# Banded attention: where the small broadcasts and the value splits stand in a unit

## The reference

```python
q = rmsnorm(q.reshape(bsz, t, 8, 64), q_norm)         # the same for k; v is taken as it is
s = einsum('bnqhd,bnkhd->bnhqk', qc, kb) * 64 ** -0.5 + bias   # own chunk + 8 chunks before it
p = softmax(where(valid, s, -1e30))
o = einsum('bnhqk,bnkhd->bnqhd', p, vb)
```

## Time and profile before

| | us |
|---|---|
| median of three runs | 1673.1 |
| lowest, highest | 1669.12, 1678.57 |
| profiled execution, its own time | 1667.27 |
| its span, first to last instruction | 1665.5 |
| TensorE busy | 1583.8 (95%) |
| DVE busy | 983.7 (59%) |
| ACT busy | 657.9 (40%) |
| GpSimd (POOL) busy | 305.2 (18%) |
| mean granted TensorE clock | 0.977 |

### The profile page before, as it was taken

One profiled execution on the slowest core, in us unless ns is written; L12 is line 12 of the kernel. 1 busy time (PEld: TensorE's weight loads), 2 busy tenths in 40 slices (PEclk: granted clock), 3 DMA queues, 4 the chain that ended last, 5 costly groups with the idle time before them and its releaser, 6 DMA issues.

```text
span 1665.5 us, 27534 instructions
## 1 busy us (share of the span) xinstructions
PE 1583.8 (95%) x11220; PEld 1550.6 (93%) x11220; DVE 983.7 (59%) x1393; ACT 657.9 (40%) x1154; POOL 305.2 (18%) x354
## 2 busy tenths in 40 slices
PE   6999999997889999997889989999999999999999
PEld 6999999996788899997779989999999899999999
DVE  6626776536778643245643486666666558646653
ACT  5521021126889522124532263333333333333332
POOL 1011000002320010003410014444444411010110
PEclk9999999988999999998999999999999999999999
DMA  7425111002110244101051223443333686354563
GB/s 241 146 90 169 42 39 39 26 1 93 37 37 33 70 156 142 39 14 51 26 183 67 78 78 145 146 145 145 145 145 147 235 295 213 91 170 147 158 211 112
DMA packets 63666, 189.37 MB, mean 114 GB/s; under 512 B 7872, under 2 KB 13048, under 8 KB 63408
## 3 DMA queue, kind: packets, MB, share of 16 engines
q1 hardware_dynamic: 37904, 91.11, 17.3%
q0 software_dynamic: 25648, 96.65, 16.3%
HBM read 138.58 MB, written 54.12 MB: 116 GB/s over the span
## 4 chain that ended last, share of the span: by engine, by line
PE 84%; DVE 5%; DMA 4%; ACT 3%; issue 3%; POOL 1%; SPq 0%; DVEq 0%; ACTq 0%; POOLq 0%
PE ps L454 33%; PE ps L2700 19%; PE ps L2721 17%; PE ps L2228 3%; PE ps L2476 3%; PE ps L483 2%; DMA a<-wdn 2%; PE ps L2599 2%; PE ps L2416 1%; PE ps L2454 1%; DVE scores L1800 1%; PE ps L505 1%; PE ps L2567 1%; PE ps L2383 1%; DVE t_lo L2083 1%
## 5 line engine op out<-in xcount | busy, mean ns | idle before, releaser
L454 PE MATMUL ps<-A_hi,w_hi 128*128 128x364 f32 x768 | 173.5, 334 | 0.0
L454 PE MATMUL ps<-A_lo,w_hi 128*128 128x364 f32 x768 | 170.3, 330 | 0.0
L454 PE MATMUL ps<-A_hi,w_lo 128*128 128x364 f32 x768 | 170.0, 329 | 0.0
L395 DVE TENSOR_TENSOR w_lo<-w_raw,w_hi 128x1024 fp32r<-128x1024 f32 x43 | 52.5, 1223 | 152.5 <-ACT w_hi L391 152.0
L391 ACT ACTIVATE w_hi<-w_raw 128x1024 fp32r<-128x1024 f32 x42 | 44.3, 1057 | 242.3 <-PE ps L454 136.3
L454 PEld LDWEIGHTS ps<-A_lo,w_hi 128*128 128x128 f32 x768 | 134.8, 190 | 0.0
L454 PEld LDWEIGHTS ps<-A_hi,w_lo 128*128 128x128 f32 x768 | 134.0, 189 | 0.0
L454 PEld LDWEIGHTS ps<-A_hi,w_hi 128*128 128x128 f32 x768 | 133.6, 190 | 0.0
L2700 PE MATMUL ps<-t_hi,wq_hi 128*128 128x272 f32 x480 | 100.1, 290 | 4.1 <-DVE hid_stage L2124 4.1
L2700 PE MATMUL ps<-t_lo,wq_hi 128*128 128x272 f32 x480 | 99.7, 289 | 0.0
L2700 PE MATMUL ps<-t_hi,wq_lo 128*128 128x272 f32 x480 | 99.6, 289 | 0.0
(11 more groups left out here) (345 smaller groups left out, 4112.4 us busy)
## 6 DMA issues: line engine op xcount, KB each, us to landing
w_raw<-slabs SPq DMA_DIRECT2D x68, 512.0 KB, 3.6
quads_d<-quad_sum POOLq DMA_DIRECT2D x64, 272.0 KB, 3.2
w_raw<-wdn POOLq DMA_DIRECT2D x32, 512.0 KB, 4.2
r_raw_a<-quads_d SPq DMA_DIRECT2D x56, 272.0 KB, 2.8
r_raw_b<-quads_d SPq DMA_DIRECT2D x56, 272.0 KB, 3.0
quads_d<-hid_stage POOLq DMA_DIRECT2D x48, 272.0 KB, 2.5
Y<-xT POOLq DMA_DIRECT2D x16, 546.0 KB, 4.2
y_d<-Y POOLq DMA_DIRECT2D x16, 546.0 KB, 3.2
```

The costliest lines, as they stand in the source:

```text
L395: e.tensor_tensor(WL[:, par], RAW[:, par], WH[:, par].bitcast(F32), ALU.subtract).then_inc(s.w_lo, 1)
L454: ins = e.matmul(PS[:, 3 * par + c, 0:CH], wt[:, wpar, w], xt[:, col:col + CH], start=(first and n == 0 and m == 0), stop=(last and n == l ...
```

## The change

The items are dealt out anew over the units, and a third place is added. On TensorE items B now stand between the values and the scores, and items C, behind the scores, hold the one broadcast (j-1, 11) in unit 0. On DVE items B stand ahead of biased. On ACT v_hi of a v item at the first place stands right behind pt_hi; rstd_heads of q moves from unit 1 to unit 0, cache_hi from unit 2 to unit 1, rstd_heads of k from unit 3 to unit 2, q_hi from unit 4 to unit 3.

| unit | before: A, B | after: A, B, C |
|---|---|---|
| 0 | -, - | -, -, 11 of the pair before |
| 1 | 11 of the pair before, 6 | -, 0, - |
| 2 | 0, 1 | 1, 2, - |
| 3 | 2, 7 | 6, 3, - |
| 4 | 3, 4 | 4, 5, - |
| 5 | 5, 8 | 7, -, - |
| 6 | -, - | 8, -, - |
| 7 | 9, - | 9, -, - |
| 8 | 10, - | 10, -, - |

```diff
@@ -560,8 +560,8 @@
                 return PT5[n % 2][x][0:rows, 0:w]
             return PT[n % 2][x][:, :, :].rearrange("p a b -> p (a b)")[0:rows, 512 * p:512 * p + w]
 
-        ITEM_A = {1: -1, 2: 0, 3: 2, 4: 3, 5: 5, 7: 9, 8: 10}
-        ITEM_B = {1: 6, 2: 1, 3: 7, 4: 4, 5: 8}
+        ITEM_A = {2: 1, 3: 6, 4: 4, 5: 7, 6: 8, 7: 9, 8: 10}
+        ITEM_B = {1: 0, 2: 2, 3: 3, 4: 5}
         YA_UNIT = (29, 30, 31)
 
         def items_a(n):
@@ -570,8 +570,6 @@
             x = ITEM_A.get(i)
             if n in YA_UNIT:
                 return [(4, n - YA_UNIT[0])]
-            if x == -1:
-                return [(j - 1, 11)] if j else []
             if x is None or (x < 9 and j == 3):
                 return []
             return [(j if x >= 9 else j + 1, x)]
@@ -580,6 +578,11 @@
 
             j, i = divmod(n, 9)
             return [(j + 1, ITEM_B[i])] if i in ITEM_B and j < 3 else []
+
+        def items_c(n):
+
+            j, i = divmod(n, 9)
+            return [(j - 1, 11)] if i == 0 and j else []
 
         def item_bank(j, x):
             return 3 if j or x >= 9 else 6 if x % 3 == 1 else 7
@@ -588,7 +591,7 @@
         for x in range(9):
             ITEM[0, x] = len(ITEM) + 1
         for n in range(N_U):
-            for it in items_a(n) + items_b(n):
+            for it in items_a(n) + items_b(n) + items_c(n):
                 ITEM[it] = len(ITEM) + 1
         ITEM[3, 11] = len(ITEM) + 1
         assert len(ITEM) == N_ITEM + 3
@@ -1205,19 +1208,16 @@
                     rec_heads(j - 1, 1)
                 if j == 4:
                     return
+                if i == 0:
+                    rstd_heads(j, 0)
                 if i == 1:
-                    rstd_heads(j, 0)
+                    cache_hi(j)
                 if i == 2:
-                    cache_hi(j)
+                    rstd_heads(j, 1)
                 if i == 3:
-                    rstd_heads(j, 1)
-                if i == 4:
                     q_hi(j)
                 if i == 5:
                     k_hi(j)
-                for _, x in items_b(n):
-                    if x >= 6:
-                        v_hi(j, x - 6)
 
             def exps(n):
                 _, cols, _ = keys(n)
@@ -1271,6 +1271,9 @@
             exps(0)
             for n in range(N_U):
                 pt_hi(n)
+                for j, x in items_a(n):
+                    if j < 4 and 6 <= x < 9:
+                        v_hi(j, x - 6)
                 if n + 1 < N_U:
                     exps(n + 1)
                 if n:
@@ -1865,13 +1868,13 @@
                 if n % 9 == 8:
                     exp_recip(n // 9, 6, 9)
                 pt_lo(n)
-                for j, x in items_a(n):
+                for j, x in items_a(n) + items_b(n):
                     item(j, x)
                 if n + 2 < N_U:
                     biased(n + 2)
                 if n == 1:
                     cache_lo(e, 0)
-                for j, x in items_b(n):
+                for j, x in items_c(n):
                     item(j, x)
                 if n == 29:
                     o_add(1)
@@ -2488,9 +2491,11 @@
                     item(j, x)
                 if n:
                     values(n - 1)
+                for j, x in items_b(n):
+                    item(j, x)
                 if n + 2 < N_U:
                     scores(n + 2)
-                for j, x in items_b(n):
+                for j, x in items_c(n):
                     item(j, x)
             values(N_U - 1)
             item(3, 11)
```

## The result

The kernel after takes 1680.9 us (median of seven runs, 1673.97 to 1684.07) against 1672.7 for the kernel before on the same chip; the ratio is 1.0056, with a 95% interval of 1.0036 to 1.0077. By the ratio it is 9.4 us slower (6.0 to 12.9), by the two medians 8.2, where 7.5 were forecast; the time forecast was 1680.6. The profiled execution of the kernel before (1667.3) is 5.4 under its median, that of the kernel after (1681.3) lies at its median, so two profiles compared show more than the medians do.

A forecast was written before the change was run, and what follows sets the result against it. TensorE, busy 95% of the span, was taken to bound the kernel. Cache split 5.3, clock 1.8 and ordinary pairs 0.4 summed to +7.5 us; on the median 1673.1 that gave 1680.6, range 1672 to 1688.

The forecast's parts named there:

- Cache split of the first pair: First pair, unit 1: ACT's cache split waits for its load and delays pt_hi(2); +5.3 us (+4.5 to +7.3).
- TensorE's gap: First pair: TensorE stands from about 401.2 to 409.9, 8.7 us, until the delayed broadcast B.
- The clock: First pair, behind TensorE's stand: the lower clock level slows scores, transposes and values; +1.8 us (0 to +4).
- The ring: Units 2 to 4: the wait before the first broadcast returns equally before the second; 0 a pair (-0.5 to +0.5).
- Rival A: Broadcast waits in the pairs really vanish, some 5 us a pair; total -3.6 us, 1669.5; chance 0.10.
- Units 0 to 2: Start of a pair: moved rstd_heads and cache split on ACT make the end of unit 2 later, +1.2 us (0.6 to 1.5).
- 5 to 8: End of a pair: unit 5 loses a wait and a broadcast, -1.3 us; v_hi on ACT adds +0.2 in units 7 and 8.
- The fourth pair: Last pair, without q, k or v items: its one moved broadcast only changes sides of a unit's border; 0.
- Rival B: Low clock holds through three score blocks (+4) and ACT's moved work costs +1.0 a pair; total +11.7 us, 1684.8; chance 0.24.
- Rival C: First pair's cache load causes no stall, only the ordinary periods count; +0.4 to +2 us, 1674; chance 0.09.

The follow-up runs named there:

- a1: Kernel after, with cache_hi of the first pair moved from unit 1 to unit 4; ratio to the kernel before 1.0032, first pair 40.5 us.
- a2: Kernel before, with cache_hi of the first pair moved from unit 2 to unit 1; ratio to the kernel before 1.0050, first pair 48.4 us.
- a3: Kernel after, with DVE's cache_lo(0) moved from unit 1 to unit 0; ratio to the kernel before 1.0026, first pair 43.1 us.
- w40: Kernel after, with 40 unused matmuls added on TensorE in unit 2 before the second broadcast; ratio to the kernel before 1.0102, first pair 48.8 us.
- b1: Kernel after, with cache_hi in unit 4 for all pairs; ratio to the kernel before 0.9990, second and third pair 38.8 us.
- b4: b1 with items B back behind the scores on TensorE and behind biased on DVE; ratio to the kernel before 0.9999.
- a4: Kernel after, with 30 unused matmuls added on TensorE in unit 2 before the second broadcast; ratio to the kernel before 1.0072, first pair 48.7 us.
- b2: b1 with DVE taking a q or k item at a unit's first place ahead of pt_lo; ratio to the kernel before 0.9946.
- c1: b2 with unit 3's v_hi and v_lo behind the first piece of pt_hi and pt_lo; ratio to the kernel before 0.9942.
- c2: b2 with item 6 at the first place of unit 1 and item 3 at that of unit 3; ratio to the kernel before 0.9967.

## Why the prediction was right

- *Cache split of the first pair, +5.3.* Right, and the main cause: a1 and a2 show it from both sides, a3 shows that it is the load's arrival. Moved by the 2.4 us that the stage starts later, pt_hi(2) came at 407.8 (said 407.7), broadcast B at 410.1 (409.9), S(4) at 411.0 (410.2); most of the 0.8 at S(4) comes with the broadcast, which takes 0.90 at the low clock. No run has the 5.3 by itself: the 7.3 measured for the first pair, less the 1.4 of the clock, leave 5.9. What was off is TensorE's gap: 7.2 us, not 8.7, since its work ahead of the gap still ran at the lower level and ended 1.7 later. That changed nothing behind it.
- *The clock, +1.8.* Right in kind, and 1.4 in size in the first pair by w40. The score block's share was right (0.9 for 0.85 said); the 0.9 for transposes and V(2) did not show in that comparison, and 0.5 came with the broadcast instead. Two of the readings behind this term say less than they were taken for. The lower level of 398 to 400, in the kernel before, is an older one: it was granted from 386 to 388 on, before the stage, where TensorE was busy 0.90 of 2 us. And the stretch of 0.54 at 523 cost nothing: that pair took 32.70 us, and in a2, where the clock was 1.00 throughout, 32.71.
- *The ring, 0 a pair.* Right: b1 against b4 differ by 0.0 and 0.2 us a pair, where -0.5 to +0.5 was the bound. Rival A is thereby false. The waits in front of the second broadcasts add up to 4.7 us in the third pair of after (2.34, 1.25, 1.11), where 3 to 4 were said: the 1.1 of cache split stand in the first of them.
- *Units 0 to 2, +1.2, and 5 to 8, -1.1; together +0.2 a pair.* The third pair of after, with a clock of 1.00 throughout, is 0.5 us longer than before's, so a little mis-sized. To its fourth transposes it is 1.2 longer, as said; units 3 and 4 add 0.2 that were not said, unit 5 gives 1.2 back (1.3 said), and units 6 to 8 add 0.4 (0.2 said). b1 shows that the 1.1 us of cache split ahead of pt_hi(2) are most of the +1.2. The fourth pair, put at 0, took 0.4 more; no run tells why. It is 33.1 in all ten kernels built on the change, broadcasts in front or behind, and 32.7 in the two with before's order (before, a2).
- *What the sum left out.* A low clock in the second pair. The forecast has the wait in unit 2 (it moved in front of the second broadcast) but not that the stand of TensorE, 1.86 before and 2.35 now, would be followed by the lower level. The windows of the kernel after, second pair:

```profile
452.00:454.00 2.00, 0.28 (x2) 0.28 (x3) 1.54 (x3) 1.98 (x8) 1.62 (x2) 0.94 0.00 0
454.00:456.00 2.00, 2.00 (x12) 1.67 (x13) 0.55 (x1) 1.38 (x2) 0.00 (x0) 0.50 0.00 0
```

This pair took 41.7, the third 39.9: 1.8 us. It is most of the 3.2 us by which the 10.7 of the profiled stage exceed the +7.5; the others are 0.2 in the first pair, 0.5 more in the second, 0.3 in the third and 0.4 in the fourth. But these 1.8 us can't all be put down to the change, for a2, which has before's order in the later pairs, lost 1.5 us in the same way; how often it comes in unprofiled runs was not measured. That the medians (8.2 and 9.4) lie nearer to the forecast than the profiled stage is in part luck: the interval of 6.0 to 12.9 holds 7.5 and 10.7 alike, and no run tells them apart. In one thing the forecast was too careful: it took 8.4 us for the least that a measurement can tell, and seven runs of each kernel kept the difference clear of zero.

By the medians the cache split is the cause from a2 (+8.4 us with that line alone) and from b1, where it stands in unit 4 in all pairs and nothing of the slowdown is left (0.9990, 0.9972 to 1.0008). a1, which takes it out of the first pair alone, is too near to the kernel after in its ratio to show by itself more than its profile does.

Rival B named the right direction for what was missing (a stand costs more by its clock), but at another place: in the first pair the low clock was paid for one score block and its broadcast only. Rival C is false by a2: one unit earlier turned 2.12 us of waiting into 6.00, and the pair grew by 7.4.

## What to carry to other kernels

When a step that waits for a DMA is moved up in an engine's list, look first at what allows that DMA to be issued, not at the slack of the engine: here the load hung on DVE work of the same unit, and all of the new wait fell on what was queued behind the step. A wait on a shared buffer moves with the place of the broadcast unless the work that releases it moves too; write out the ring before and after, and then take out of it what doesn't belong in it (pt_lo ahead of the read cost 2 us a pair). The same order of the change, with the cache split in unit 4 and the read first, is 0.5% faster than the kernel before.

## What the runs showed of the hardware

Pauses of equal length had different ends. In the kernel before TensorE was busy 0.38 of 2 us in unit 2 of the second pair and kept the upper level; in a2, the same work in the third pair, it was busy 0.38 of 2 us and lost it. Windows of before, and then of a2:

```profile
440.00:442.00 2.00, 0.38 (x4) 0.14 (x3) 1.09 (x4) 1.98 (x5) 0.00 (x0) 1.00 0.00 0
442.00:444.00 2.00, 2.00 (x20) 1.87 (x21) 1.30 (x3) 1.95 (x8) 0.00 (x0) 1.00 0.00 0
```

```profile
488.00:490.00 2.00, 0.38 (x4) 0.15 (x2) 1.10 (x4) 1.98 (x5) 0.00 (x0) 1.00 0.00 0
490.00:492.00 2.00, 2.00 (x11) 1.77 (x10) 1.32 (x3) 1.39 (x5) 0.00 (x0) 0.50 0.00 0
```

The third pair of a2 took 40.9 us, that of before 39.4: the same pause cost 1.5 us more. The Trainium skill has a reason that fits, on the page "TensorE: Matmul & The Clock Gate", Part 1: the window in which TensorE's activity is watched is free-running and is not reset when a kernel starts, so it matters where in it the work lands. The runs here show the different ends, not the cause. Over the second and third pairs of the twelve profiles: with 2.34 or 2.35 us of waiting in unit 2 (after, a1, a3, a4, w40) the lower level followed in six pairs of ten, with 1.86 (before, a2) in one of four, and with 1.26 at most in front of any broadcast (b1, b2, b4, c1, c2) in none of ten, whose mean clock is 1.00. The seven pairs with it are 0.5 to 1.9 us longer than their like without it. Ten, four and ten pairs of one execution each show a tendency, no threshold.

A low stretch doesn't always cost time. In the fourth pair, whose mean clock is 0.95 in before and 1.00 in a2, the length is 32.70 and 32.71 us; in after (0.95) and b1 (1.00) it is 33.10 and 33.12.
